# Two transformer blocks in one kernel: weight blocks of the last stage loaded earlier and shared, and its order of steps rewritten

## What is computed

```python
y = mix_branches(...)                       # two gated branches, then @ w_out
x_new = x + gt1 * rmsnorm(y, g_post_mix)
h2 = modulate(rmsnorm(x_new, g_pre_ffn), sh2, sc2)
q = rmsnorm((h2 @ w_query).reshape(T, 8, 2, 128))     # 8 heads, two halves
s = einsum('thpd,pnd->thpn', q, sub_keys)             # 128 keys in each half
s1, i1 = top_k(s[:, :, 0], 16);  s2, i2 = top_k(s[:, :, 1], 16)
best, pos = top_k(s1[..., :, None] + s2[..., None, :], 16)
gate = softmax(best)
act = gelu(einsum('td,thkd->thk', h2, u_tab[idx])) * gate
out = einsum('thk,thkd->td', act, v_tab[idx])         # 16 rows per token and head
x = x_new + gt2 * rmsnorm(out, g_post_ffn)
```

## Time and profile before

| | us |
|---|---|
| median of three runs | 2205.35 (2205.13 to 2205.49) |
| the profiled execution, its own time | 2205.23 |
| its span, first to last instruction | 2203.4 |
| PE busy | 1490.9 (68%) |
| DVE busy | 753.4 (34%) |
| ACT busy | 434.0 (20%) |
| POOL busy | 291.8 (13%) |
| DMA, mean over the span | 370 GB/s, 814.24 MB |

### The profile page before, as it was taken

How to read it: one execution, slowest core, us unless ns; L and a number is a source line. 1 busy time by engine, 2 the same in 40 slices (tenths; PEclk the granted TensorE clock), 3 DMA queues, 4 the chain that set the end, 5 groups by cost and what they waited for, 6 DMA issues and landing times.

```text
span 2203.4 us, 24558 instructions
## 1 busy us (share of the span) xinstructions
PE 1490.9 (68%) x10272; PEld 620.2 (28%) x10272; DVE 753.4 (34%) x1892; ACT 434.0 (20%) x992; POOL 291.8 (13%) x265
## 2 busy tenths in 40 slices
PE   8888766767775665666659999997756744344344
PEld 7554311322221111111114454555323511001000
DVE  5823101000000000000013143345657676876774
ACT  1321110000000000000011174342333232323221
POOL 0000000000000000000000000003434445444341
PEclk9988877888898878777879999998867865655555
DMA  9549999999999999999994346449999999999996
GB/s 387 210 174 397 427 426 426 426 428 427 427 427 427 427 427 426 427 427 427 427 418 162 152 185 235 178 166 410 422 421 402 419 420 420 417 420 419 419 419 279
DMA packets 75870, 814.24 MB, mean 370 GB/s; under 512 B 8464, under 2 KB 8592, under 8 KB 9840
## 3 DMA queue, kind: packets, MB, share of 16 engines
q1 hardware_dynamic: 38704, 544.03, 59.3%
q0 software_dynamic: 36864, 268.45, 29.4%
...
HBM read 811.40 MB, written 1.05 MB: 369 GB/s over the span
## 4 chain that ended last, share of the span: by engine, by line
DMA 48%; PE 33%; DVE 12%; ACT 4%; issue 2%; POOL 2%; ACTq 0%; DVEq 0%; POOLq 0%
DMA AR<-in_w_down 18%; DMA AR<-in_w_up 15%; DMA AR<-in_peer_uv,AR 14%; PE PS L396 13%; DVE AR L1384 3%; PE PS L624 3%; PE PS L829 3%; PE PS L645 2%; PE PS L787 2%; PE PS L407 2%; POOL AR L1761 2%; PE PS L511 1%; DVE AR L906 1%; DVE AR L908 1%; PE PS L657 1%
## 5 line engine op out<-in xcount | busy, mean ns | idle before, releaser
L1761 POOL DMA_INDIRECT AR<-in_peer_uv,AR x256 | 290.0, 1133 | 1704.9 <-DVE AR L1375 1438.3
L829 PE MATMUL PS<-AR 32*32 32x512 f32 x4096 | 233.2, 944 | 328.8 <-ACT AR L1720 328.8
L624 PE MATMUL PS<-AR 128*32 128x512 f32 x2048 | 301.9, 726 | 187.1 <-DMA AR<-in_w_up 131.9
L1384 DVE CUSTOM_DVE_ANT_0 AR<-AR 128x1024 f32<-128x1024 f32 x256 | 309.5, 1222 | 154.1 <-DMA AR<-in_peer_uv,AR 154.1
L396 PE MATMUL PS<-AR 128*128 128x512 f32 x736 | 330.8, 605 | 1.9 <-DVE AR L881 1.9
L645 PE MATMUL PS<-AR 128*32 128x512 f32 x1024 | 174.7, 818 | 102.4 <-DMA AR<-in_w_down 94.9
L1080 DVE TENSOR_TENSOR AR<-AR,PS 128x512 f32<-128x512 f32 x16 | 11.0, 688 | 596.6 <-PE PS L624 596.6
L396 PEld LDWEIGHTS PS<-AR 128*128 128x128 f32 x736 | 140.1, 195 | 173.2 <-issue 172.6
L624 PEld LDWEIGHTS PS<-AR 128*32 128x32 f32 x2048 | 63.2, 121 | 414.2 <-DMA AR<-in_w_up 207.5
L829 PEld LDWEIGHTS PS<-AR 32*32 32x32 f32 x4096 | 43.9, 128 | 474.1 <-ACT AR L1720 461.7
L1094 DVE COPY AR<-PS 128x512 f32<-128x512 f32 x16 | 11.1, 692 | 282.9 <-PE PS L645 282.9
...
## 6 DMA issues: line engine op xcount, KB each, us to landing
AR<-in_w_gate SPq DMA_DIRECT2D x64, 2048.0 KB, 26.1
AR<-in_w_up SPq DMA_DIRECT2D x64, 2048.0 KB, 25.7
AR<-in_w_down SPq DMA_DIRECT2D x64, 2048.0 KB, 26.4
AR<-in_w_in SPq DMA_DIRECT2D x29, 2048.0 KB, 7.8
AR<-in_w_ada SPq DMA_DIRECT2D x12, 2048.0 KB, 9.8
AR<-in_peer_w_query SPq DMA_DIRECT2D x8, 2048.0 KB, 11.9
AR<-in_w_out SPq DMA_DIRECT2D x6, 2048.0 KB, 11.5
AR<-in_w_branch_sgu SPq DMA_DIRECT2D x4, 2048.0 KB, 7.7
```

The costliest lines, as they stand in the source:

```text
L624: x = pe.matmul(PS[32 * q:32 * q + 32, bk, :], XS[:, j, e * 32:(e + 1) * 32], IN[key][:, jj, q * 512:(q + 1) * 512], start=(j == 0), stop= ...
L829: x = pe.matmul(PS[c:c + 32, ACC[a][g], :], DI[t, p, r, :], AR[t, off + 1024 + m * 512:off + 1536 + m * 512], start=(h == 0 and p == 0), s ...
L1384: v.tensor_tensor_reduce(rows, rows, HB[:, a, :], 1.0, 0.0, MULT, ADD, DOT[:, ix, k:k + 1]).then_inc(*w.hit("dot", ix, k))
L1761: pool.indirect_dma_start(out=AR[:, off:off + 2048], out_offset=None, in_=D["peer_uv_2"], in_offset=bass.IndirectOffsetOnAxis(ap=EI[:, ix, ...
```

## The change

Weights: w_ba(0,1), w_ba(1,1) and w_op(0,1) get slots of their own at W0, o and o+16384, loaded once the last attention values are done; the later blocks w_op(1,1), wq(2,0), wq(3,0), wq(0,1), wq(1,1) share the slots at W0 and o+16384. wq(2,.) and wq(3,.) serve both halves. The rows in turn take all four ring slots (eight places) and o+21120 from the start, o+2048 from yt(1) on, and three more at pair 8.

Order: steps of two engines are split into a part for each (ht/hte, yt/yte, ft/fte, qm/qme, qs/qse, back/bke, gain1/gain1p/gain1e), and `late` is written out with the row after which each part comes. The routing parts follow rows 0, 1, 3, 4, 6 and 9 of a pair.

Norm: the scores are ranked straight from PSUM, and the 16 + 16 best values are multiplied by the query's factor later, in rt3. ACT does the second half of the turn of h4.

```diff
-        place = [...] + [W0, SPARE, o + 21120, o + 14336]
+        place = [...] + [W0, SPARE, o + 21120, o + 14336, o, o + 16384]
...
-            steps(pairs[1], h[2], [("gain1",)])
+            steps(pairs[1], [("ht", 0), ("hte", 0), ("gain1",)])
             filler(then)
-            steps(pairs[2], *b[0], pairs[3], *b[1], pairs[4])
+            steps(pairs[2], [("ba", 0, 0), ("bae", 0, 0), ("gain1p",), ("gain1e",)], pairs[3], [("ba", 1, 0), ("bae", 1, 0)], pairs[4])
...
-            late = queries(2, 0) + queries(3, 0) + [h[0], h[1] + h[2]]
-            late += [b[0][0], b[0][1] + b[1][0], b[1][1] + y[0], p[0][0], p[0][1] + p[1][0], p[1][1] + u[0], u[1] + u[2], u[3] + u[4]]
-            late += queries(0, 1) + [[("gain2",)], [("back", 1)]] + queries(1, 1) + queries(2, 1) + queries(3, 1)
-            todo += [("take", 0), ("qm", 0, 0), ("qs", 0, 0), ("rt0", 0)]
...
-            todo += [(f"rt{s}", 0) for s in range(1, 6)]
+            todo += [("take", 0), ("qm", 0, 0), ("qme", 0, 0), ("rt0", 0), ("qs", 0, 0), ("qm", 1, 0), ("rt1", 0), ("rt2", 0), ("qse", 0, 0),
+                     ("qme", 1, 0), ("qs", 1, 0), ("back", 0), ("bke", 0), ("rt3", 0), ("rt4", 0), ("rt5", 0),
+                     ("qse", 1, 0)]
             filler(then)
             filler(then)
+            todo += [("qm", 2, 0), ("qme", 2, 0), ("qs", 2, 0), ("qm", 3, 0), ("qme", 3, 0), ("qs", 3, 0)]
+            late = {4: [("hn1", 1)], 6: [("hn2", 1), ("ht", 1)], 11: [("hte", 1), ("ba", 0, 1)], 14: [("ba", 1, 1)], 16: [("bae", 0, 1)],
+                    19: [("bae", 1, 1), ("yt", 1)], 23: [("yte", 1), ("op", 0, 1)], 26: [("op", 1, 1)], 28: [("ope", 0, 1)],
+                    31: [("ope", 1, 1)], 33: [("up1", 1)], 35: [("up2", 1)], 37: [("fn1", 1)], 39: [("fn2", 1), ("ft", 1)], 43: [("fte", 1)],
+                    78: [("back", 1)], 82: [("bke", 1), ("gain2",), ("gain2p",)], 87: [("gain2e",)], 3: [("qse", 2, 0), ("qse", 3, 0)]}
+            for n, *x in ((30, 4, 0), (33, 5, 0), (46, 4, 1), (49, 5, 1), (52, 6, 0), (55, 6, 1), (58, 7, 0), (61, 7, 1),
+                          (64, 0, 1), (67, 1, 1), (70, 2, 1), (73, 3, 1)):
+                late.setdefault(n, []).append(("qm", *x))
+                late.setdefault(n + 3, [])[:0] = [("qme", *x), ("qs", *x)]
+                late.setdefault(n + 6, [])[:0] = [("qse", *x)]
...
-                if n % 3 == 0 and late:
-                    todo += late.pop(0)
-                if k == 0 and ix < 15:
-                    routes += [(f"rt{s}", ix + 1) for s in range(6)]
-                if (k % 2 or ix == 0) and routes:
-                    todo.append(routes.pop(0))
+                todo += late.pop(n, [])
+                if k in (0, 1, 3, 4, 6, 9) and ix < 15:
+                    todo.append((f"rt{(0, 1, 3, 4, 6, 9).index(k)}", ix + 1))
...
-            free = {k: ("mm", "av", 15) for k in (o + 2048, W0 + 2048, o + 16384, o + 18432)}
-            free[o + 21120] = ("gsb", 1, 1)
-            free.update({k: ("used", "wq", i, 0) for i in range(2) for k in halves[i]})
+            free = {o + 21120: ("gsb", 1, 1)}
+            for i, event in ((0, ("wq", 0, 0)), (2, ("w_bs", 0, 1)), (3, ("w_bs", 1, 1)), (1, ("wq", 1, 0))):
+                free.update({k: ("used", *event) for k in halves[i]})
...
             def ffn_turn(a):
-                turn("scaled", "h4", XN[:, a, :], True, a, ("xn5", a))
+                turn("scaled", "h4", XN[:, a, :], True, a, ("xn5", a), second="moved")
...
             def qm(h, a):
-                key = ("wq", n, a)
+                key = ("wq", n, a if n < 2 else 0)
...
-            def rt0(ix):
-                a, h = work[ix]
-                rq = RQ[:, a, 2 * h:2 * h + 2]
-                rstd1(("q", ix), rq, rq, 128, 1e-6, ("rq", h, a))
-                rstd2(("q", ix), rq)
+            def query_mean(h, a):
+                w.wait_ge("mm", "rq", h, a)
+                v.tensor_scalar(RQ[:, a, 2 * h:2 * h + 2], PS[:, banks.at("rq", h, a), 0:2], 1.0 / 128, 1e-6, MULT, ADD).then_inc(
+                    *w.hit("mean", ("q", 8 * a + h), also=[("rq", h, a)]))
             def rt1(ix):
...
+                score = [PS[:, banks.at("rsc", ix), q * 128:(q + 1) * 128] for q in range(2)]
+                w.wait_step()
+                for q in range(2):
+                    w.step(v.max(SV[:, q, 0:8], score[q]))
...
             def rt3(ix):
+                rstd2(("q", ix), rq)
+                w.wait_ge("rstd", ("q", ix))
+                w.step(v.tensor_tensor(SV, SV, rq.unsqueeze(2).broadcast_to([128, 2, 16]), MULT))
...
+                    for n in range(2):
+                        square(("wq", n, 0), "peer_w_query_2", n)
+                    w.wait_ge("mm", "av", 15)
+                    for slot, key, name, n in ((NS, "w_ba", "w_branch_attn_2", 0), (NS + 4, "w_ba", "w_branch_attn_2", 1),
+                                               (NS + 5, "w_op", "w_out_2", 0)):
+                        load(slot, (key, n, 1), weight(name, n), 8, 512)
+                    turn[0], ids[0] = 0, [NS, NS + 5]
...
-                elif stage == "qm" and x[0] % 2 == 0:
+                elif stage == "qm" and (x in ([4, 0], [6, 0]) or x[0] in (0, 2) and x[1] == 1):
                     square(("wq", x[0] // 2, x[1]), "peer_w_query_2", x[0] // 2)
```

More of the change, by code:

```diff
@@ L217, in build @@
         ACC = [[0, 1, 2, 3], [4, 5, 6, 7]]
-        place = [NARENA + i * SLOT for i in range(NS)] + [W0, SPARE, o + 21120, o + 14336]
+        place = [NARENA + i * SLOT for i in range(NS)] + [W0, SPARE, o + 21120, o + 14336, o, o + 16384]
         IN = {}
@@ L260, in mixer_order @@
             assert not first
-            def tail(a):
-                return [[("hn1", a)], [("hn2", a)], [("ht", a)]], [[[("ba", n, a)], [("bae", n, a)]] for n in range(2)], \
-                    [[("yt", a)]], [[[("op", n, a)], [("ope", n, a)]] for n in range(2)], \
-                    [[("up1", a)], [("up2", a)], [("fn1", a)], [("fn2", a)], [("ft", a)]]
             pairs = []
@@ L331, in mixer_order @@
                     todo.append(("row", ix, k))
-                if n % 3 == 0 and late:
-                    todo += late.pop(0)
-                if k == 0 and ix < 15:
-                    routes += [(f"rt{s}", ix + 1) for s in range(6)]
-                if (k % 2 or ix == 0) and routes:
-                    todo.append(routes.pop(0))
+                todo += late.pop(n, [])
+                if k in (0, 1, 3, 4, 6, 9) and ix < 15:
+                    todo.append((f"rt{(0, 1, 3, 4, 6, 9).index(k)}", ix + 1))
                 if k % 2:
                     todo.append(("act", ix, k // 2))
-            assert not late and not routes
+            assert not late
             return todo
         ORDER = mixer_order()
+        HEADS = [tuple(x) for stage, *x in ORDER if stage == "qm"]
         RING = [5, 2, 3, 4]
@@ L788, in qm @@
                                       HT[:, j, a * 128:(a + 1) * 128], start=(j == 0), stop=(j == 7))
-                x.then_inc(*w.hit("mm", "qp", h, a, also=[("used", *key)] if r else ()))
+                x.then_inc(*w.hit("mm", "qp", h, a, also=[("used", *key)] if r and (n < 2 or a) else ()))
             def qs(h, a):
@@ L795, in qs @@
                 for q in range(2):
-                    x = pe.matmul(PS[:, b, q:q + 1], SQP[:, h % 2, q * 128:(q + 1) * 128], ones[:, 0:1], start=True, stop=True)
+                    x = pe.matmul(PS[:, b, q:q + 1], SQP[:, HEADS.index((h, a)) % 2, q * 128:(q + 1) * 128], ones[:, 0:1], start=True, stop=True)
                 x.then_inc(*w.hit("mm", "rq", h, a))
@@ L1237, in row_of @@
                     w.wait_ge("mm", "av", 15)
+                    w.wait_ge("used", "wq", 1, 1)
                     for m in range(2):
@@ L1420, in vector @@
             mine = {"rope": rope, "zn1": zn1, "zn2": zn2, "zn3": zn3, "zmix": zmix, "ga": ga, "gs": gs, "bs": bs, "exp": att_exp,
-                    "cmb": att_combine, "gain1": lambda: row_of("g1", G1, COL[:, 3, :]), "gain2": lambda: row_of("g2", G2, COL[:, 4, :]),
-                    "hn1": hn1, "hn2": hn2, "ht": heads_turn, "bae": bae, "ope": ope, "up1": up1, "up2": up2, "fn1": fn1, "fn2": fn2,
+                    "cmb": att_combine, "gain1": lambda: row_of("g1", COL[:, 3, :]), "gain2": lambda: row_of("g2", COL[:, 4, :]),
+                    "gain1e": lambda: row_copied("g1", G1), "gain2e": lambda: row_copied("g2", G2),
+                    "hn1": hn1, "hn2": hn2, "hte": heads_turn, "bae": bae, "ope": ope, "up1": up1, "up2": up2, "fn1": fn1, "fn2": fn2,
                     "norm_turn": norm_turn,
-                    "ft": ffn_turn, "rt0": rt0, "rt1": rt1, "rt2": rt2, "rt3": rt3, "rt4": rt4, "row": row, "rt5": rt5, "leave": leave}
+                    "fte": ffn_turn, "qse": query_mean, "rt1": rt1, "rt2": rt2, "rt3": rt3, "rt4": rt4, "row": row, "rt5": rt5, "leave": leave}
             for stage, *x in ORDER:
@@ L1690, in qm @@
                 w.wait_ge("qp", h, a)
-                if (h, a) not in ((0, 0), (1, 0)):
```

(8 more changed lines are left out.)

114 lines of the change are left out of this document (47 added, 67 removed).

## The result

| | before | after |
|---|---|---|
| median of four runs, us | 2205.24 (2203.62 to 2205.49) | 2175.6 (2174.04 to 2180.99) |
| the profiled execution, its own time | 2205.23 | 2176.36 |
| its span | 2203.4 | 2174.5 |
| first gather in the span | 1486.21 | 1478.71 |
| from the first gather to the end | 717.2 | 695.8 |

The ratio is 0.9871, with a 95% interval from 0.9854 to 0.9889. The forecast was 2177. I call the last line of the table the **last stage**. It was 21.4 us shorter, and it began 7.5 us earlier; together that is the 28.9 us of the span.

The account below looks back on a forecast made before the run. PE sets the time before about 1487 us, DMA bytes behind it. Terms -24.9 + 0 - 5.9 - 0.9 - 1.1 + 7 - 2.5 = -28.3 from 2205.2 gave 2177 us, range 2169 to 2191.

Parts of the forecast that it names:

- (c): Row of gain 1, ahead of the rows: PE's wait and slow matmuls there go, -5.9 us (bounds -3 and -6).
- (d): Turn of h4 before the first query: ACT does the second half beside DVE, -0.9 us (bounds 0 and -0.9).
- (e): First head's routing: scores ranked from PSUM ahead of the query norm, -1.1 us, nothing in later heads.
- (f): Start of the rows: nine places and late V steps, no longer hidden by blocks, cost +7 us (0 to +20).
- (a): Weight blocks among the rows of the last stage: five fewer at 4.98 us each, -24.9 us.
- (b): Three early blocks after av 15: loaded in the empty DMA window before the first gather, 0 us (bounds 0 and +5).
- (g): DMA dip from 1665 to 1680: goes with the root asked for steps ahead, -2.5 us (bounds 0 and -2.5).
- (h): Two places for late blocks among the rows: blocks land before they are wanted, 0 us.
- The feared wait at cmb 10: Ahead of the rows: DVE's gain-row copies stand ahead of cmb 10, which could eat the gain-row saving.
- The start was fed: Denies the rival that the first 40 rows starve, the start gap costing 20 us, not 7: 2190 us, chance 0.19.
- The early loads were early: Denies the rival that the three early blocks land among the rows after all: +15, 2192 us, chance 0.06.
- PE never waited for a late block: Denies the rival that late blocks stop the release of rows: slower, about 2213 us at 40 each, chance 0.03.

Follow-up runs that it names:

- e1: The changed kernel with wq(2,.) and wq(3,.) loaded once for each token half again: 2185.75 us, ratio to before 0.9911.
- e4: The changed kernel with the row of gain 1 made in one piece again, ahead of z(1,1): 2182.41 us, ratio to before 0.9903.
- e6: The changed kernel with both halves of the turn of h4 scaled by DVE as before: 2175.49 us, ratio to before 0.9869.
- e5: The changed kernel with the query norm applied to the scores ahead of the ranking again: 2176.99 us, ratio to before 0.9878.
- e2: The changed kernel with the three early blocks loaded only once the first pair's indices are there: 2185.01 us, ratio to before 0.9903.
- e3: The changed kernel with wq(2,.) and wq(3,.) loaded per token half and the three early blocks held until the first pair's indices: 2192.46 us, ratio 0.9941.
- e8: The changed kernel with the whole routing of pair 1 (rt0 to rt5) moved ahead of the first row: 2182.64 us, ratio to before 0.9898.
- e10: The changed kernel with pair 1's routing ahead of the first row, its scores (rt0) behind the first bs: 2174.22 us, ratio to before 0.9865.

## Why the prediction was right, and where it wasn't

The time fell 28.9 us by the profiled executions (29.6 by the medians) and 28.3 were forecast. That is closer than the terms deserve. (c), (d) and (e) together promised 7.9 us and gave 7.2, and (f) charged 1 to 1.5 us more than it cost, so the misses partly cancel; and the first gather alone moves by 4 us between profiles of one kernel. What was right is the mechanism and the size of the large terms; the last microsecond is luck. By the terms:

| term | predicted | measured | by |
|---|---|---|---|
| (a) five fewer blocks | -24.9 | -24.9 | 4.98 a block (e1), and five issues by SP behind the first gather instead of ten blocks |
| (b) early loads | 0 | 0 | the DMA engines done with them at 1478.5 |
| (c) gain row | -5.9 | -6.2 to -6.3 | e4; profiles |
| (d) turn of h4 | -0.9 | 0 | e6 |
| (e) scores first | -1.1 | -0.7 to -1.0 | e5; profiles |
| (f) start gap | +7 | +5.5 to +6.1 | windows of both kernels; e2 |
| (g) dip | -2.5 | -2.6 | e3 |
| (h) late blocks | 0 | 0 | no wait of PE for in_peer_w_query |

**(a) and (b)** stood. In SP's order ten blocks behind the first gather became five, and the stage answered by bytes alone: with the 5.5 us of new gap, -24.9 + 5.5 - 2.6 = -22.0, measured -21.4. What is left of 0.6 no run here places. av 15 ended at 1462.13 (1462.6 predicted), and the DMA engines were done with the early blocks at about 1478.5 (1479.5).

The Trainium skill (DMA: Bandwidth & Descriptors, Where 436 GB/s comes from) puts the bound of loads from HBM at about 358 GB/s for a core, and names beside it a measured 425 GB/s for a transfer of 16 MB. The runs disagree with the bound and agree with the measured figure, with 419 to 428 GB/s held over hundreds of microseconds on this one core, and 9.95 us for the two blocks of e1, where 358 GB/s would give 11.7.

**(c)** was the surest term ahead of the rows, because both its parts, the wait of 4.42 and the stretch from 1.95 to 3.46, could be read in the earlier trace rows, and e4 gave both back. The feared wait at cmb 10 didn't come.

In the two profiles, transposes of the heads to transposes of the FFN input are 1371.00 to 1465.17 before (94.17 us) and 1370.71 to 1458.59 after (87.88): 6.3 us. From there the first query starts 0.1 us later than before, and the first gather follows it 1.0 sooner (e); with 0.3 us that lie ahead of the transposes of the heads this makes the 7.5 by which the first gather came earlier. These are the rows of before at either end:

```profile
1371.00 1.09 PE L384 MATMUL PS<-PK,AR 128*128 128x128 f32 x8
...
1465.17 1.73 PE L384 MATMUL PS<-PK,AR 128*128 128x128 f32 x8 [2.62 <-DVE AR L1302]
```

**(d) is the term that was mis-sized.** I let ACT's half "run beside DVE's two operations", ending with av 15. It does run beside them, but it starts 2.01 us after the transposes begin, 1460.60, lasts 1.50 and ends at 1462.10; PE is free at 1462.13 and starts the query 0.91 later. DVE alone gave the same 0.91. In e6 DVE's last operation of the turn ends at 1462.43, and the query starts 0.55 us behind it; with ACT it starts 0.94 behind the turn's end, and before it was 0.69. Only the distance from the end of av 15's matmuls is the same 0.91 each time, and in two profiles of the unchanged kernel the row names no releaser (issue). So the end of the turn is not what PE stood for, and the prediction took the 0.91 for a wait that a faster turn would end. What the 0.91 is made of no run here separates. The bound I had given, 0, was the value.

**(e)** came out at 0.7 to 1.0. From the first query's matmuls to the first gather it was 16.69 us before and 15.67 after; undoing the edit gave back 0.7. The root's wait, put behind the ranking, was still 0.27 us, and the small multiply 0.19.

The Trainium skill (VectorE: DVE Perf Modes, The TRN2 errata) gives a PSUM source about twice the fixed cost of an SBUF source. These rows don't show it: two MAX8 take 0.49 us from either, and FIND_INDEX8 0.29 from PSUM and 0.28 from SBUF.

**(f)** is the term that the forecast hung on, and it was worked out from the right mechanism: nine places, each freed by a bs, a query or a V step, and V steps every 5.46 us where 5.0 would do. The first three intervals were 5.6, 5.7 and 7.3, and the eight V steps of head 0 took 5.8 in the mean. The 2 us for ba(0,1) were put on the wrong step. Its matmuls run from 1524.40, behind the fifth V step, and the DMA engines carry 411 GB/s or more in every 5 us from 1525 to 1560. What was late is the fourth V step, at 1518.82, for which PE waited 3.40 us for ACT; the window of 192 GB/s follows it. The size of (f) came out in part by that exchange. The runs also add what I hadn't seen, that DVE's routing of pair 1 makes the spacing (e8, e10: 3.7), and that moving it mostly moves the gap in front of the first V step.

**(g)** went as said. e3 doesn't separate it from the rest of the new order, but the windows put 2.6 of its 2.9 us where the dip was.

**The rivals.** The start was fed (6.7 us missing, not 20). The early loads were early; e2 shows what it would have meant had they not been, 2185, and not the 2192 I gave, because I had charged 15 us and the gap would have given 6 of it back. PE never waited for a late block. That rival's price was also added up wrongly: 40 us a block is 2 us in each of five blocks above the 38 that make the gain vanish (33 us), so about 2220 and not 2213. PE did get two waits from 1480 to 1840 that before doesn't have, for banks of PSUM that DVE's query mean holds:

```profile
PE PS L781 <- DVE AR L1299: 5.9, 1, 5.9
PE PS L772 <- DVE AR L1299: 5.3, 1, 5.3
```

They stand at 1652.6 and 1685.7 and cost nothing, since the DMA engines are full there (419 GB/s from 1600 to 1660, 419 from 1680 on). e8 shows the same wait in front of a bs, where it does cost.
